# Attention values weighed transposed, and half tiles, rotations, sums and first scores moved in the order of a one-core transformer stack

## What is computed

```python
for i in range(4):                                   # first block
    # A: indexer + top-64 keys per query, B: three dilations shared per head, C: causal attention
    q, k, v, ..., qm = split_cols(x @ w_in[i])       # 12 heads of 64; B: 4 value heads of 192
    mix = attention_of_kind(rope(q), rope(k), v)
    mo  = softmax(qm @ mk.T / 8) @ mv                # 4 heads over 256 memory rows
    mixed = concat(mix, mo) @ w_out[i]
    x = layer_norm(ALPHA * x + mixed)
    x = layer_norm(ALPHA * x + (silu(x @ w_gate) * (x @ w_up)) @ w_down)
for i in range(2):                                   # second block
    h = rms_norm(x) * (1 + scale) + shift            # modulated by c @ w_ada
    rq, rk, rv, rg, sq, sk, sv, sg = split(h @ w_in_2[i])
    y = concat(retention(rot(rq), rot(rk), rv) * silu(rg),
               stick_breaking(sq, sk, sv) * silu(sg)) @ w_out_2[i]
    x = x + gate * y
out = rms_norm(x)
```

## Time and profile before

| | |
|---|---|
| median of three runs | 1695.37 us (1690.32 to 1695.37) |
| the profiled execution | 1693.71 us, of which the span from first to last instruction is 1691.9 us |
| PE busy with matmuls | 1613.1 us, 95% of the span |
| DVE / ACT busy | 1061.3 us (63%) / 721.5 us (43%) |
| mean granted TensorE clock | 0.982 |
| DMA | 299.89 MB, 177 GB/s on average |

### The profile page before, as it was taken

One profiled execution on the slowest core, in us unless ns is written; L12 is line 12 of the kernel. 1 busy time (PEld: TensorE's weight loads), 2 busy tenths in 40 slices (PEclk: granted clock), 3 DMA queues, 4 the chain that ended last, 5 costly groups with the idle time before them and its releaser, 6 DMA issues. The chain is left out here.

```text
span 1691.9 us, 20176 instructions
## 1 busy us (share of the span) xinstructions
PE 1613.1 (95%) x8388; PEld 1337.0 (79%) x8388; DVE 1061.3 (63%) x1439; ACT 721.5 (43%) x862; POOL 52.8 (3%) x89
## 2 busy tenths in 40 slices
PE   6899999999999999999999999999999989999998
PEld 5898788888777878878788888787888868787876
DVE  5575667566566765575667656857676575557635
ACT  4435444433443433445443443454433434444352
POOL 2000000000000000000000000000100010000000
PEclk9799999999999999999999999999999989999999
DMA  8552257654523766352466744413756435334420
GB/s 262 190 203 100 101 205 271 231 215 161 196 98 139 274 222 250 129 220 76 145 240 225 262 165 170 156 74 129 278 224 260 173 148 197 125 122 148 167 111 25
DMA packets 45035, 299.89 MB, mean 177 GB/s; under 512 B 5444, under 2 KB 5700, under 8 KB 11280
## 3 DMA queue, kind: packets, MB, share of 16 engines
q1 hardware_dynamic: 38736, 278.48, 44.9%
q0 software_dynamic: 5776, 19.01, 3.6%
q10 hardware_dynamic: 432, 1.11, 0.2%
HBM read 296.20 MB, written 2.65 MB: 177 GB/s over the span
## 5 line engine op out<-in xcount | busy, mean ns | idle before, releaser
L824 PE MATMUL psum<-w_high,xt_high 128*128 128x512 f32 (+1 forms) x1472 | 581.0, 395 | 20.8 <-DVE xt_low L1339 12.7
L1145 ACT ACTIVATE w_high<-w_raw 128x2048 fp32r<-128x2048 f32 x241 | 458.8, 1905 | 287.9 <-DMA w_raw<-in_weights 176.2
L1313 DVE TENSOR_TENSOR w_low<-w_raw,w_high 128x2048 fp32r<-128x2048 f32 x241 | 546.7, 2272 | 53.0 <-ACT w_high L1145 52.3
L826 PE MATMUL psum<-w_high,xt_low 128*128 128x512 f32 (+1 forms) x1472 | 568.9, 387 | 0.0
L825 PE MATMUL psum<-w_low,xt_high 128*128 128x512 f32 (+1 forms) x1472 | 568.0, 386 | 0.0
L824 PEld LDWEIGHTS psum<-w_high,xt_high 128*128 128x128 f32 x1472 | 281.1, 191 | 88.9 <-issue 12.3
L826 PEld LDWEIGHTS psum<-w_high,xt_low 128*128 128x128 f32 x1472 | 280.4, 191 | 56.7
L825 PEld LDWEIGHTS psum<-w_low,xt_high 128*128 128x128 f32 x1472 | 281.4, 191 | 51.5
L1606 DVE TENSOR_TENSOR arena<-arena,psum 128x256 f32<-128x256 f32 x88 | 37.0, 420 | 215.9 <-ACT arena L1236 215.5
L824 PE MATMUL psum<-w_high,ht_high 128*128 128x512 f32 x352 | 141.5, 402 | 0.0
L826 PE MATMUL psum<-w_high,ht_low 128*128 128x512 f32 x352 | 138.2, 393 | 0.0
(11 more groups left out here) (221 smaller groups left out, 1642.5 us busy)
## 6 DMA issues: line engine op xcount, KB each, us to landing
w_raw<-in_weights SPq DMA_DIRECT2D x263, 1024.0 KB, 4.8
norm_params<-in_ln_g POOLq DMA_DIRECT2D x8, 512.0 KB, 4.1
norm_params<-in_ln_b POOLq DMA_DIRECT2D x8, 512.0 KB, 5.7
kv_outside<-arena POOLq DMA_DIRECT2D x3, 512.0 KB, 2.9
mem_kv<-kv_outside POOLq DMA_DIRECT2D x3, 512.0 KB, 3.5
norm_params<-mods_outside POOLq DMA_DIRECT2D x3, 512.0 KB, 6.4
x_rows<-in_x SPq DMA_DIRECT2D x2, 512.0 KB, 8.8
w_raw<-in_weights SPq DMA_DIRECT2D x2, 512.0 KB, 6.2
```

Source lines behind the costliest of these rows:

```text
L824: e.matmul(dst, a_hi, b_hi, start=first, stop=False)
L826: return e.matmul(dst, a_lo, b_hi, start=False, stop=last)
L1145: e.activation(K.w_hi[:, g % RING, 0:w], K.w_raw[:, r, 0:w], ACT.Copy).then_inc(K.high.hit(t), 1)
L1313: e.tensor_tensor(K.w_lo[:, s, 0:w], K.w_raw[:, r, 0:w], K.w_hi[:, s, 0:w].bitcast(F32), ALU.subtract).then_inc(K.taken.hit(t), 1)
```

## The change

1. **Values turned.** `weigh` on PE makes the values as stationary operand (strips of 64 columns, on either half of the output's partitions) and moves the transposed probabilities (128 columns), so that the result comes transposed. ACT copies it to `mixed_t` (a new `weigh` in its program), and the DVE part is dropped. `recip` on DVE now multiplies the whole row of probabilities by the reciprocal before `turn_prob`, which waits for that (`shared_out`). The transposes of `mixed` on PE are gone: `xt` of the mix reads `mixed_t`, and is added by halves, at earlier hooks.
2. **One more half tile.** Layer 3's `first_columns` and the first groups of the two layers of the second block take one more half tile (`more`) into the part of each row block, in a bank of the ring of wide places. In the second block's groups, `late` moves from behind the third to behind the fifth product.
3. **In front of the low halves.** Rotations use `on_first` (the background step, then `split`), the last sum of `w_out` and the sums of the last row block of each feed-forward come before `split`, in layer 0 the transposes of row block 1 come before the hook's `split`. In the last layer, `rms` and `modulate` of row block 0 come between products (`last_downs`), and its first transposes after the last of them.
4. **Sticks.** Pair 0's `sb_scores` are added two products earlier; its `sb_keep` and `sb_later` stay in their hook.
5. Smaller ones: a hook lies between the transposes of the indexer's queries and of its keys, and between the rotation of `rk` and the transpose of `rq`; in kind B two iterations of attention follow each other once more in the group of `w_out`; the memory's rows are transposed by halves; one copy of layer 0 goes from ACT to DVE.

```diff
@@ Plan
+    def on_first(self):
+        self.step_background()
+        self.split()
 def block(...):
             for rb in range(RB):
-                if late and rb and not half:
-                    late()
                 self.gemm(t, rb, half, gen, "gemm", uses[rb])
                 if half:
                     then(rb, uses[rb], t)
+                if late and not rb and not half:
+                    late()
                 self.on()
 def group(self, blocks, gen, after, prompt=False, more=None):
+            if more:
+                uses_more.append(self.wide.take())
+                self.gemm(t_more, rb, 0, gen, "wide", uses_more[rb], prompt=prompt)
+                after[rb][-1]()
+        if more:
+            self.second_half(more, gen, uses_more)
 def indexer_work(self, layer):
             self.turn("qi", layer, rb, range(4), "act")
+        yield
         for rb in range(RB):
             self.turn("ki", layer, rb, range(1), "act")
 def feed_forward(self, layer):        # rb 1: hooks of the last four products
+                elif step == FF_STEPS - 1:
+                    if layer == LAST:
+                        self.next_rows(layer, 0)
+                elif layer == LAST:
+                    self.last_downs(step)
             for h in range(2):
                 self.add("residual", Residual(out, rb, h, t[FF_STEPS - 1], "wide", acc[rb], h == 1))
+            if rb:
+                self.split()
             self.norm(out, rb)
+    def last_downs(self, step):
+        if step == FF_STEPS - 3:
+            self.low()
+            self.add("rms", (0, 0))
+            self.ahead()
+            self.add("modulate", (0, 0))
+        else:
+            self.ahead()
 def first_columns(more):              # layer 3
                 if rb == 0:
                     late()
-                self.split()
+                else:
+                    self.beside(self.indexer_work(layer))
+                self.on()
+                self.gemm(t_more, rb, 0, gen, "wide", uses_more[rb], prompt=True)
+                self.on()
 def attention(...):
+        def first_turned():
+            self.xt(mix, 0, (0,))
+            self.on()
         def turned():
-            self.xt(mix, 0)
+            self.xt(mix, 0, (1,))
 def stick_work(self, layer):
+        pairs = [self.stick_breaking(layer, n) for n in range(SB_H // 2)]
+        next(pairs[0])
         yield
         yield
-        yield from self.pipelined([self.stick_breaking(layer, n) for n in range(SB_H // 2)])
+        yield from self.pipelined([self.begun(pairs[0]), *pairs[1:]])
 def second_layer(self, layer):
-        self.group([proj(0), proj(1)], gen, [[self.split, self.split, late, queries], [self.on] * 3 + [keys]])
-        project(2)
+        self.group([proj(0), proj(1)], gen, [[self.split] * 3 + [rotations(0), rows], [self.on] * 3 + [rotations(1), self.on]],
+                   layer == 0, proj(2))
@@ tensor_program, weigh
-                m = e.matmul(psum[:, to, n * w:n * w + w], K.probt[slot][:, c * P:c * P + P], rows[:, kb, c0:c0 + w],
-                             start=kb == 0, stop=kb == nk // P - 1)
+                        m = e.matmul(psum[p0:p0 + HD, to, (chunk - first) * P:(chunk - first) * P + P], rows[:, kb, c0:c0 + HD],
+                                     K.probt[slot][:, c * P:c * P + P], start=kb == 0, stop=kb == nk // P - 1)
@@ scalar_program
+    def weigh(j):
+        act.wait_ge(*K.turned.at(j.out))
+        if first % 2:
+            e.activation(to[HD:P, first // 2, :], bank[HD:P, 0, :], ACT.Copy)
+        if last % 2 == 0:
+            e.activation(to[0:HD, last // 2, :], bank[0:HD, last // 2 - first // 2, :], ACT.Copy)
+        e.activation(to[:, a:z, :], bank[:, a - first // 2:z - first // 2, :], ACT.Copy).then_inc(K.tr.sem(j.out), 1)
@@ vector_program, recip
+        pr = pr.rearrange("p (h k) -> p h k", k=nk)
+        e.tensor_tensor(pr, pr, K.recip[:, slot, 0:n].unsqueeze(2).broadcast_to([P, n, nk]),
+                        ALU.mult).then_inc(K.shared_out.hit(j.n), 1)
```

More of the change, by code:

```diff
@@ L134 @@
 Gemm = namedtuple("Gemm", "tile rb half gen ring use kind")
-Evac = namedtuple("Evac", "where rb use tile silu by")
+Evac = namedtuple("Evac", "where rb use tile silu by ring")
 Xt = namedtuple("Xt", "gen rb g use after")
@@ L269, in group, with second_half, then @@
                     after[rb][len(blocks) * half + n]()
+            if more:
[4 more added lines that the diff above has]
+            self.second_half(more, gen, uses_more)
+    def second_half(self, block, gen, uses):
+        t = self.tile(*block[:4], 4)
+        for rb in range(RB):
+            self.gemm(t, rb, 1, gen, "wide", uses[rb])
+            block[-1](rb, uses[rb], t, "wide")
+            self.on()
     def evacuate(self, where, silu=False, by=("act", "dve")):
-        def then(rb, use, tile):
+        def then(rb, use, tile, ring="gemm"):
             self.blocks[where, rb] = use
-            self.add("evac", Evac(where, rb, use, tile, silu, by[rb]))
+            self.ring_of[where] = ring
+            self.add("evac", Evac(where, rb, use, tile, silu, by[rb], ring))
         return then
@@ L552, in first_layer, with memory_rows, then @@
             project(0)
-            narrow([self.split] * 2)
             self.drain()
+            def memory_rows(rb):
+                def then():
+                    self.xt(("mem",), rb, (0,))
+                    self.split()
+                return then
+            narrow([memory_rows(rb) for rb in range(RB)])
             self.beside(self.indexer_work(layer))
@@ L631, in out_and_forward, with units_on, first_rows, last_rows @@
         late = []
-        def rest():
+        def units_on():
+            self.on()
+            if KINDS[layer] == "B":
+                self.step_background()
+        def first_rows():
+            self.xt(mix, 1, (0,))
+            self.on()
+        def last_rows():
             self.on()
@@ L636, in rest @@
             assert self.units[layer, 1][-1].kind == "mem"
-            self.xt(mix, 1)
+            self.xt(mix, 1, (1,))
+        def rest():
+            self.split()
             self.norm(key, 0)
@@ L1082, in sb_scores @@
         for what in ("sq", "sk"):
-            pe.wait_ge(*K.gemms.out(plan.blocks[(what, j.layer), j.pair // 2]))
+            pe.wait_ge(*K.made((what, j.layer), j.pair // 2))
         pe.wait_ge(*K.wide.free(j.wide))
@@ L1230, in turn_prob @@
                              ACT.Copy).then_inc(K.tr.sem(use), 1)
+    def weigh(j):
+        work = strips(j)
+        first, last = work[0][0], work[-1][0]
+        act.wait_ge(*K.turned.at(j.out))
+        a, z = (first + 1) // 2, (last + 1) // 2
+        to, bank = K.mixed_t[j.rb], psum[:, K.tr.place(j.out), :].rearrange("p (c s) -> p c s", s=P)
+        if first % 2:
[3 more added lines that the diff above has]
+        e.activation(to[:, a:z, :], bank[:, a - first // 2:z - first // 2, :], ACT.Copy).then_inc(K.tr.sem(j.out), 1)
     def gate(j):
@@ L2069, in evac_from @@
     def evac_from(self, j):
-        bank = self.psum[:, self.gemms.place(j.use), :]
+        bank = self.psum[:, self.ring(j.ring).place(j.use), :]
         return bank.rearrange("p (n c) -> p n c", n=2) if j.where[0] in ("mem", "tail", "sq", "sk") else bank
@@ L2074, in evac_scale, with left_from, ring, made @@
         return SB_D ** -0.5 if where[0] == "sq" else HD ** -0.5 if where[0] == "tail" and rb else 1.0
+    def left_from(self, j):
+        if j.after:
+            return self.mixed_t[j.rb][:, 4 * j.g:4 * j.g + 4, :]
+        return self.psum[:, self.tr.place(j.use), :].rearrange("p (c s) -> p c s", s=P)
+    def ring(self, name):
+        return self.gemms if name == "gemm" else self.wide
+    def made(self, where, n):
+        return self.ring(self.plan.ring_of.get(where, "gemm")).out(self.plan.blocks[where, n])
+    def left_made(self, gen, rb, g):
+        return self.mixed_low.at((gen, rb, g)) if gen[0] == "mix" else self.tr.out(self.plan.xt_uses[gen, rb, g])
     def turn_source(self, what, rb, layer):
```

209 lines of the change are left out of this document (110 added, 99 removed).

## The result

The changed kernel took 1733.8 us (median of four runs, 1731.9 to 1734.7). The kernel before took 1693.2 us beside it (four runs). The ratio is 1.0237, with a 95% interval of 1.022 to 1.0254. The profiled executions have spans of 1730.1 and 1691.9 us, so 38.2 us have to be found. I had forecast 1705 and a range up to 1718.

A forecast was written before the change was run, and what follows sets the result against it. PE was taken as the bound, through its work, waits and clock. Terms +24.3 (values turned), +8.5 (clock), +2 (kind B) and -24.0 (gains) sum to +10.8 on 1693.71, giving 1705 us; range 1686 to 1718.

The forecast's parts named there:

- The order on ACT: Attention of A and C layers: PE waits for ACT's copy behind exponentials, +10.4 a layer; net +8.1, +24.3 for three.
- The clock: Attention of layers 0, 2 and 3: two more half-clock stretches per layer at 1.7 us, less one existing: +8.5.
- The rival for this: The clock falls behind every new wait: 30 in place of +8.5, total 1719 us, chance 0.12.
- `weigh` on PE: Kind B: 72 matmuls of 128 columns replace 24 of 192, +2.4; A and C keep their pace, nothing.
- The gains: Steps moved in front of the lows, and the rest, cut PE's waits: sum -24.0.
- The opening: Kernel's start: layer 0's half tiles and transposes no longer stand behind a low, -5, of -14 to -2.
- the indexer's -6.2: Indexer's turns in two hooks: four waits, 4.5 us, and one fall of the clock, 1.7, go.
- The rotations of the first block: Rotations ahead of low in the first block: 6.4 us of waits go, a part returns: -5.
- Those of the second block: Rotations ahead of low in the second block: 4.9 us of waits and falls go, some returns: -4.2.
- the second block's first group: A fifth product needs a late w_low: wait about 7.7 for 4.7, +1.5, and +1.0 next layer: +2.5.
- The sticks: Pair 0's earlier scores gain 0: sb_keep stays behind the hook's low, so waits of 3.52 and 3.45 us stay.
- Kind B: Layer of kind B: fewer transposes and waits against a longer iteration and weigh, +2, of -1 to +8.

The follow-up runs named there:

- the first experiment: Changed kernel with ACT's copy of the weighed values in front of the new unit's exponentials, not behind them: 1685.1 us, ratio to before 0.9948.
- the three-wait run: Kernel before, DVE's weigh step also waiting for the new unit's exponentials in three iterations of each of layers 0, 2 and 3: 1715.4 us, ratio 1.0139.
- Parts 2 to 5 alone: Changed kernel without its first part (values turned), the mix transposed whole and at the old places: 1685.5 us, ratio to before 0.9943.
- the waits stood all through the attention: Kernel before, DVE's weigh step also waiting everywhere until ACT has finished the exponentials of the unit just added: 1747.3 us, ratio 1.0315.
- four edits of the order: Changed kernel with ACT's copy first, first-block rotations behind the low, first sb_keep before the low, attention's steps before low and high: 1665.9 us, ratio 0.983.
- The three later edits: Each alone on the 1685.1 us kernel with ACT's copy first: first-block rotations behind low 1676.0; first sb_keep before low 1676.9; attention's steps before low and high 1673.4.
- the one with added matmuls: Changed kernel with each unit's weigh matmuls run three times, the same result written again: 1728.8 us, ratio 1.0208.

## Why the prediction was wrong, point by point

- **The order on ACT** was the right mechanism. Forecast for the iterations of an A or C layer: waits +10.4. In layer 3 they sum to 1.61 + 2.34 + 2.33 + 2.01 + 2.30 + 2.78 + 2.01 = 15.4 where before had 2.6 in seven waits: +12.8. Iterations 2 to 5 and 7 came out within 0.5 of the forecast; the rest is iteration 6, 5.1 in two waits in place of 4.0. That this was the main cause the first experiment shows: 48.7 us.
- **The clock** was the step that failed most. I gave the new waits in the attention of layers 0, 2 and 3 six stretches of half clock, two a layer, where there had been one: +8.5. There were sixteen, a double one counted twice, 47.4 us outside waits in place of 3.4: +22.0. I had counted a fall behind some six of eleven waits of this length, and then took fewer for the new ones, because one stretch would cover two waits. It didn't: behind the two waits of each sixth iteration stands a double stretch of 6.8 us (194.7, 832.9, 1184.5). Over the whole kernel I had a net of +3.4, with three falls taken away elsewhere; it was +23.6. That waits close together bring falls more often fits the three-wait run and the count over all traces; what makes one fall and another not stays open. The rival for this was priced at 30 and stood at 0.12, but its total, 1719, leaned on the gains below.
- **`weigh` on PE** I had at +2.4 in kind B, and there it was +2.3 (4.2 us for 24 matmuls, 6.5 for 72). Elsewhere I had it at nothing, and it was -15, so -13 in all. I took the pace of the old form, 0.107 each, as the nearest row. The strips of 64 columns in turn on either half of the output run at 0.067: twelve from 1159.55 to 1160.35, against twelve in 1.29 us. That page of the Trainium skill, "TensorE: Matmul & The Clock Gate", Part 3, has matmuls on different column tiles overlapping; the trace agrees. By their starts the two halves of a pair begin 0.005 to 0.008 us apart, and pair follows pair after 0.11. In kind B, where strips on the same half follow one another (from 477.21), one follows the other after 0.109.
- **The gains** (-24) were too high. Parts 2 to 5 alone are -9.7. To place them in the changed kernel I took the distance between it and the kernel before at the same products, by count.
  - The opening gained 5.4 us by 116 us. But 3.8 of that are the indexer's wait of 2.10 at 70.6 and the fall behind it, which stood in the next term; the opening itself gave about 1.6 of its 5.
  - Of the indexer's -6.2 these 3.8 came. In layer 3 the wait of 2.10 at 1062.6 came back as two for DVE, 0.44 and 1.22.
  - The sums of `w_out` came as forecast (2.3 gone), and so did layer 3's first columns (4.0 by 1051, for 3.8).
  - The rotations of the first block cost instead of giving. Those of the second block came as forecast: 2.9 us of waits and the fall at 1415.6 are gone, 4.6 for 4.2.
  - The earlier `modulate` won 10 us and the second block's first group gave all of it back: the distance was 41.9 at 1366, 31.8 at 1393 and 41.9 at 1411. `w_low` ends at 1432.6 and PE waits 6.67, then 1.07 for `xt_low`; 7.7 was the forecast of that wait.
- **The sticks** were right: 3.52 and 3.46 stayed, and the cause was the `low` in front of `sb_keep`.
- **The transposes** were right: 7.8 us gone.
- **Kind B** (+2) grew by 7.4 us from its first scores to the last sum of `w_out`, with three stretches of half clock where none had been.

## What to carry to other kernels

When a buffer's release moves to another engine, read what stands in front of it in *that* engine's order, and follow the chain up to the first thing that can't start early; here two swapped steps were worth 3% of the kernel. Price several short waits in a row with the clock. What it cost here for each us waited was 0.74 where the waits stood all through the attention, 0.68 in the changed kernel and 0.26 with three in a row. A lone wait isn't free either: 33 of 77 had a fall. An edit that takes work away can be judged only after its order is mended: the changed kernel was 2.4% slower than before in one order, 0.5% faster in a second and 1.7% faster with four edits of the order. And it is to be held against the other parts without it: those gave as much as the second order did, so that the turned form pays at all isn't shown. The three later edits were not tried on the old form.

## What I had not expected of the hardware

Span less PE waits less half of the half clock outside them is almost a constant. It is 1593 to 1596 us in the six kernels that weigh the old way, and 1572 to 1576 in the six that weigh turned (the one with added matmuls aside). So what differs between kernels of one form is PE's waits and its clock, within 4 us.

Waits of 1.6 to 2.4 us brought a fall in 33 of 43 cases where another of over 1 us stood in the 13 us before them, and in 33 of 77 where none did. The Trainium skill describes such swinging under "A second HAM failure mode: psum-queue depth-cycling" on the page named above; these traces agree, with 26 separate stretches of half clock in the changed kernel in place of 11, and add that waits close together bring it more often.

And 48 us of useless matmuls, most of them in waits, took no more time than the changed kernel did without them.
